# Router scores in a fused transformer block: two of the four groups of merged query weights kept as two rounded parts

## The reference

```python
h   = x * (1 + scale1) + shift1
z   = h @ w_in
# mixer A: gated 128x128 spatial MLP; mixer B: latent attention, 4 heads, up to 1152 keys
x   = LN1(alpha * x + gate1 * (concat(A, B) @ w_o))
h2  = x * (1 + scale2) + shift2
q   = (h2 @ w_pq).reshape(T, 8, 2, 128)
s   = einsum('thsd,hskd->thsk', q, sub_keys)      # 16 lists of 128 scores for each token
# top 16 of each list, top 16 of the 256 sums per head -> 128 of 16384 experts, softmax weights
x   = LN2(alpha * x + gate2 * sum_k w_k * gelu(u_k . h2) * v_k)
```

## Time and profile before

| | |
|---|---|
| runs before | 3253.39, 3255.07, 3258.79 us, median 3255.07 |
| the profiled execution | 3245.81 us, span 3244.0 us |
| PE busy over the span | 3159.9 us (97%) |
| DVE, ACT, POOL busy | 2594.7 (80%), 1253.2 (39%), 1617.1 us (50%) |
| mean granted TensorE clock | 0.992 |
| transfers | 979.82 MB, mean 302 GB/s |

### The profile page before, as it was taken

The page is one execution under the profiler, slowest core; times in us unless marked ns, Lnnn a source line. Parts: engine busy times, 40 slices in busy tenths (PEclk is TensorE's granted clock), DMA queues, the critical chain, the costliest instruction groups (busy, mean ns, idle before and its releaser), DMA issues.

```text
span 3244.0 us, 43176 instructions
## 1 busy us (share of the span) xinstructions
PE 3159.9 (97%) x15522; PEld 2625.2 (81%) x15522; DVE 2594.7 (80%) x5188; ACT 1253.2 (39%) x2305; POOL 1617.1 (50%) x1031
## 2 busy tenths in 40 slices
PE   8999899999988899999999999999999999999998
PEld 5887566665545699999999989989999999999997
DVE  3333138888889799999999889889999998888876
ACT  3343344333436633333343333333343333333343
POOL 0300113788777588888888887223333332233310
PEclk9999999999999999999999999999999999999999
DMA  6934866777677899999999999989899999999963
GB/s 248 390 117 159 326 221 195 208 220 193 198 214 227 283 349 348 349 351 356 351 339 349 357 358 387 370 337 370 340 371 362 352 366 356 354 364 357 345 227 118
DMA packets 300866, 979.82 MB, mean 302 GB/s; under 512 B 94580, under 2 KB 148724, under 8 KB 241399
## 3 DMA queue, kind: packets, MB, share of 16 engines
q1 hardware_dynamic: 159256, 532.10, 44.9%
q0 software_dynamic: 141120, 444.94, 39.4%
q10 hardware_dynamic: 288, 0.16, 0.0%
HBM read 902.22 MB, written 74.87 MB: 301 GB/s over the span
## 4 chain that ended last, share of the span: by engine, by line
PE 41%; POOL 18%; issue 3%; DVE 2%; DMA 1%; ACT 0%; DVEq 0%; ACTq 0%
PE scores L1952 21%; PE bank L1962 17%; POOL g_cells L189 12%; POOL ring L1914 6%; PE scores L1962 4%; DMA work<-in_u 1%; DVE ring L2100 0%; DVE uL L2283 0%; DVE acc L2117 0%; DMA ring<-in_uv,slots 0%; DVE vL L2279 0%; DVE slots L2222 0%; DVE ga L2296 0%; DVE st L2249 0%; DVE cL L2274 0%
## 5 line engine op out<-in xcount | busy, mean ns | idle before, releaser
L1914 POOL DMA_INDIRECT ring<-in_uv,slots x384 | 569.1, 1482 | 793.0 <-DVE carry L2117 695.1
L189 POOL DMA_INDIRECT g_cells<-slots x384 | 726.7, 1893 | 225.7 <-issue 115.9
L1952 PE MATMUL scores<-hR,uR 128*128 128x384 f32 x2032 | 682.2, 336 | 6.2 <-DVE uL L2283 6.2
L1952 PE MATMUL scores<-hR,uL 128*128 128x384 f32 x2032 | 682.0, 336 | 0.0
L1952 PE MATMUL scores<-hL,uR 128*128 128x384 f32 x2032 | 680.6, 335 | 0.0
L2039 ACT ACTIVATE cR<-ga 128x384 fp32r<-128x384 f32 x253 | 133.1, 526 | 942.8 <-PE bank L1962 547.6
L2100 DVE CUSTOM_DVE_ANT_0 ring<-ring,slots 128x1024 f32<-128x1024 f32 x384 | 467.5, 1254 | 17.6 <-DMA ring<-in_uv,slots 17.6
L1962 PE MATMUL bank<-vR,cR 128*128 128x512 f32 x1265 | 414.6, 392 | 0.0
L1962 PE MATMUL bank<-vR,cL 128*128 128x512 f32 x1265 | 412.7, 391 | 0.0
L1962 PE MATMUL bank<-vL,cR 128*128 128x512 f32 x1265 | 411.2, 390 | 0.0
L1952 PEld LDWEIGHTS scores<-hR,uR 128*128 128x128 f32 x2032 | 381.5, 188 | 18.4 <-DVE uL L2283 8.8
(11 more groups left out here) (370 smaller groups left out, 4593.9 us busy)
## 6 DMA issues: line engine op xcount, KB each, us to landing
work<-in_v SPq DMA_DIRECT2D x256, 512.0 KB
work<-in_u SPq DMA_DIRECT2D x254, 512.0 KB
work<-pq_scratch SPq DMA_DIRECT2D x36, 2048.0 KB
work<-in_w_o SPq DMA_DIRECT2D x18, 2048.0 KB
g_cells<-work POOLq DMA_DIRECT2D x48, 512.0 KB, 5.5
work<-g_cells SPq DMA_DIRECT2D x32, 768.0 KB
work<-g_blocks SPq DMA_DIRECT2D x31, 768.0 KB
g_blocks<-big SPq DMA_DIRECT2D x8, 2048.0 KB
```

The costliest lines, as they stand in the source:

```text
L189: pool.indirect_dma_start(out=cells_of(g_dram, i), out_offset=bass.IndirectOffsetOnAxis(ap=slots[:, i, D + k:D + k + 1].bitcast(U32), axis=0),
L1914: pool.indirect_dma_start(out=ring[:, k % R, :], out_offset=None, in_=a["uv"], in_offset=bass.IndirectOffsetOnAxis(ap=ids[:, k // P, k % P ...
L1952: mm = pe.matmul(A[t][:, 0:CW], w[t][:, k, :], h[:, k, :], start=(k == 0 and w is uR and h is hR), stop=(k == DK - 1 and w is uL))
```

## The change

Groups 2 and 3 of the merged weights (`SPLIT`) are no longer kept as float32 but as two fp32r parts. ACT copies each merged block rounded, DVE subtracts the rounded block from the same PSUM bank and only then frees the bank; POOL writes both parts to memory, a group being two halves of 2 MB, each with both parts of four blocks. A tile's transposed `h2` is split in the same way at h=0 of its tile i-2 (`parts`: ACT rounds, DVE subtracts). `score(i, 2)` and `score(i, 3)` then use 24 fp32r products in place of 8 float32 ones, the first 12 with one half, the others with the second. Each half is a number of its own in `WEIGHTS`, with the wait taken by the whole score that it follows. The staging of the merge has 8 buffers for groups 0 and 1, and 6 pairs for groups 2 and 3. The five reads of `mix_scratch` for tiles 2 to 6, which SP issued in slot 0 ahead of the keys, x and the first merge weights, are issued in slot 4, after the loads of `mix(0)`. A few waits for the merge's writes are added at first uses of the shared space (left out below).

```diff
+SPLIT = (2, 3)
...
+        pq_dram = [nc.dram_tensor("pq_scratch", [4, P, DK * 512], F32, kind="Internal").ap(),
+                   nc.dram_tensor("pq_parts", [len(SPLIT), 2, P, DK * 512], F32, kind="Internal").ap()]
...
+            w_parts = nc.alloc_sbuf_tensor_at("w_parts", [P, 2 * DK * 512], F32R, offset=work_at)
...
+            if key[0] == "score" and key[2] in SPLIT:
+                WEIGHTS.append((*key, 1))
...
+        merged = [front[:, at:at + 512] for at in (
+            *range(4 * D, 6 * D, 512), *range(9 * D, 10 * D, 512), *range(11 * D, 12 * D, 512))]
+        merged += [carry[:, at:at + 512] for at in range(0, 2 * D, 512)]
+        xR, xL = (x[:, :] for x in x_parts)
+        wp = w_parts[:, :].rearrange("p (b r c) -> p b r c", b=2, r=2)
...
+        MERGED = [0, 32, 64, 128, 192]
...
-                        sp.wait_ge(w_mm, W[WEIGHTS[at - 2]] + 1)
+                        sp.wait_ge(w_mm, W[WEIGHTS[at - 2][0:3]] + 1)
                     if key[0] == "score" and key[1] == 0:
                         for m_out in merged_out:
-                            sp.wait_ge(m_out, FILLED + 2 * (key[2] + 1) * 16)
+                            sp.wait_ge(m_out, FILLED + MERGED[key[2] + 1])
+                    if key[0] == "score" and key[2] in SPLIT:
+                        sp.dma_start(w_parts[:, at % 2 * DK * 512:(at % 2 + 1) * DK * 512].bitcast(F32),
+                                     pq_dram[1][SPLIT.index(key[2]), len(key) - 3, :, :]).then_inc(wr_in[at % 2], 16)
+                        return
                     part = key[1] if key[0] == "merge" else key[-1]
-                    src = {"mod": a["w_mod2"], "mix": a["w_o"], "merge": a["w_pqT"], "score": pq_dram}[key[0]]
+                    src = {"mod": a["w_mod2"], "mix": a["w_o"], "merge": a["w_pqT"], "score": pq_dram[0]}[key[0]]
...
-                        for t in range(2, LAST):
-                            sp.dma_start(slots[:, t, :], mix_dram[t, :, :]).then_inc(tile_in[2], 16)
...
+                    if n == H:
+                        for t in range(2, LAST):
+                            sp.dma_start(slots[:, t, :], mix_dram[t, :, :]).then_inc(tile_in[2], 16)
...
                     if h == 1 and 0 <= i - 2 < NT:
                         load("score", i - 2, 2)
+                        load("score", i - 2, 2, 1)
                     if h == 2 and 0 <= i - 2 < NT:
                         load("score", i - 2, 3)
+                        load("score", i - 2, 3, 1)
...
+                for g in range(4):
+                    for k in range(DK):
+                        pool.wait_ge(*emptied("merge", g, k))
+                        if g in SPLIT:
+                            for r_ in range(2):
+                                at = r_ * 4 * 512 + k % 4 * 512
+                                pool.dma_start(pq_dram[1][SPLIT.index(g), k // 4, :, at:at + 512],
+                                               merged[2 * (k % 6) + r_]).then_inc(merged_out[k // 2], 16)
+                        else:
+                            pool.dma_start(pq_dram[0][g, :, k * 512:(k + 1) * 512], merged[k]).then_inc(merged_out[k // 2], 16)
...
+                    if g in SPLIT:
+                        ps = bank("score", i, g)
+                        pe.wait_ge(x_low, i + 1)
+                        for half in range(2):
+                            at = WEIGHTS.index(("score", i, g, 1) if half else ("score", i, g)) % 2
+                            weights("score", i, g, *range(1, half + 1))
+                            for k in range(4):
+                                kk, sl = 4 * half + k, slice(k * 512, (k + 1) * 512)
+                                left = slice(kk * P, (kk + 1) * P)
+                                pe.matmul(ps[:, :], xR[:, left], wp[:, at, 0, sl], start=(kk == 0), stop=False)
+                                pe.matmul(ps[:, :], xR[:, left], wp[:, at, 1, sl], start=False, stop=False)
+                                mm = pe.matmul(ps[:, :], xL[:, left], wp[:, at, 0, sl], start=False, stop=(kk == DK - 1))
+                        mm.then_inc(w_mm, 1)
+                        return
...
                     for k in range(DK):
                         ps, f = bank("merge", g, k)
-                        x = DK * g + k
-                        if x >= 4:
-                            act.wait_ge(merged_out[x % 4], FILLED + x // 4 * 16)
-                        act.activation(merged[:, x % 4, :], ps[:, :], ACT.Copy).then_inc(f, 1)
+                        if g and k == 0:
+                            for m_out in merged_out:
+                                act.wait_ge(m_out, FILLED + MERGED[g])
+                        if g in SPLIT:
+                            if k >= 6:
+                                act.wait_ge(merged_out[0], FILLED + MERGED[g + 1])
+                            act.activation(merged[2 * (k % 6)].bitcast(F32R), ps[:, :], ACT.Copy).then_inc(merged_high, 1)
+                        else:
+                            act.activation(merged[k], ps[:, :], ACT.Copy).then_inc(f, 1)
+
+                def parts(i):
+                    if i == 0:
+                        act.wait_ge(w_mm, W["merge", 3, DK - 1] + 1)
+                    else:
+                        act.wait_ge(w_mm, W["score", i - 1, 3] + 1)
+                    act.activation(xR, slots[:, i, 0:D], ACT.Copy).then_inc(x_high, 1)
...
+                    if h == 0 and 0 <= i - 2 < NT:
+                        parts(i - 2)
...
+                def merge(g):
+                    for k in range(DK):
+                        w = W["merge", g, k]
+                        dve.wait_ge(merged_high, SPLIT.index(g) * DK + k + 1)
+                        dve.tensor_tensor(merged[2 * (k % 6) + 1].bitcast(F32R), PS[6 + w % 2][:, :], merged[2 * (k % 6)],
+                                          ALU.subtract).then_inc(free[w % 2], 1)
+
+                def parts(i):
+                    dve.wait_ge(x_high, i + 1)
+                    dve.tensor_tensor(xL, slots[:, i, 0:D], xR.bitcast(F32), ALU.subtract).then_inc(x_low, 1)
...
+                    if h == 0 and 0 <= i - 2 < NT:
+                        parts(i - 2)
                     if h == 0 and i >= 3:
                         decode(i - 3)
...
+                    if n in MERGE and MERGE[n] in SPLIT:
+                        merge(MERGE[n])
```

More of the change, by code:

```diff
@@ L161, in build @@
                 ("hR1", D, big_at, KT * H * P + 4 * 512), ("hL1", D, big_at, KT * H * P + 6 * 512))]
+            x_parts = [nc.alloc_sbuf_tensor_at(name, [P, D], F32R, offset=front_at + 4 * word) for name, word in (("xR", 0), ("xL", D))]
+            w_parts = nc.alloc_sbuf_tensor_at("w_parts", [P, 2 * DK * 512], F32R, offset=work_at)
             ga = nc.alloc_sbuf_tensor_at("ga", [P, 2, CW], F32, offset=big_at + 4 * KT * H * P * 2)
@@ L168, in build @@
             lists_of = middle(nc, a, sb, sem, PS, ident, modc, sp1, silu, slots, carry, work, first_in, big, krT, kT, vv, front, mod_in, x1_dram, gate_dram, g_dram, placed,
-                              mix_dram, tile_in, tile_out, a_mm, a_ev, g_in, ga, pq_dram, pool_out, scores_ps)
+                              mix_dram, tile_in, tile_out, a_mm, a_ev, g_in, ga, pq_dram, pool_out, scores_ps, x_parts, w_parts)
         experts(nc, a, sb, sem, PS, slots, carry, work, first_in, lists_of, x1_dram, g_dram, gate_dram, placed, a_mm, a_ev, g_in, ga, big_at)
@@ L716, in mixer_inputs, with middle @@
     return pool_out
-def middle(nc, a, sb, sem, PS, ident, modc, sp1, silu, slots, carry, work, first_in, big, krT, kT, vv, front, mod_in, x1_dram, gate_dram, g_dram, placed, mix_dram, tile_in, tile_out, a_mm, a_ev, g_in, ga, pq_dram, merged_out, scores_ps):
+def middle(nc, a, sb, sem, PS, ident, modc, sp1, silu, slots, carry, work, first_in, big, krT, kT, vv, front, mod_in, x1_dram, gate_dram, g_dram, placed, mix_dram, tile_in, tile_out, a_mm, a_ev, g_in, ga, pq_dram, merged_out, scores_ps, x_parts, w_parts):
     NH = NT * H
@@ L859, in middle @@
         w_mm, const_in, x1_out, gate_out = (sem(f"b_{n}") for n in ("wmm", "const", "x1out", "gateout"))
+        x_high, x_low, merged_high = (sem(f"b_{n}") for n in ("xhigh", "xlow", "mghigh"))
         row_in, x_in = ([sem(f"b_{n}{k}") for k in range(2)] for n in ("rowin", "xin"))
@@ L1310, in score @@
                         act.wait_ge(listed, 4 * (i - 1) + g + 1)
+                    elif g == 0:
+                        for m_out in merged_out:
+                            act.wait_ge(m_out, FILLED + MERGED[4])
                     act.activation(s[:, 4 * g:4 * g + 4, :], ps[:, :].rearrange("p (l k) -> p l k", l=4),
@@ L1320, in spread @@
                         for m_out in merged_out:
-                            act.wait_ge(m_out, FILLED + DK * 16)
+                            act.wait_ge(m_out, FILLED + MERGED[4])
                     sl = slice(4 * g, 4 * g + 4)
@@ L1580, in decode @@
                 def decode(i):
+                    if i == 0:
```

(2 more changed lines are left out.)

2 lines of the change are left out of this document (removed).

## The result

The changed kernel takes 3315.48 us (median of 4, 3310.52 to 3318.66) against 3254.70 us (median of 4): ratio 1.0185, 95% interval 1.017 to 1.0199, so 60.8 us slower. The forecast was 3291.6 us with a range up to 3312. The profiled execution took 3317.99 us with a span of 3315.8 us, 71.8 us above the span shown before.

A forecast was written before the change was run, and what follows sets the result against it. PE was taken to bound the experts, DVE and PE in turn tiles 3 to 8. Terms 18 + 1.5 + 26 - 9 = +36.5 us on 3255.07 gave 3291.6 us, range 3259 to 3312 (forecast's own 3280 to 3303).

The forecast's parts named there:

- `score(i, 3)` ... No wait: Steady tile: both halves of this score's weights arrive before they are wanted, at 694.7 and 699.7, so PE does not wait.
- the line behind it: Steady tile: next score(0) has its weights at 710.9 or 712.7 and starts at 711.0 or 712.7, against 709.28 before.
- The step above: Steady tile: score(i, 2) has its second half at 683.1, wanted at 683.9, and ends at 686.6.
- The split of x: Tiles 3 to 8: ACT's rounding and DVE's subtraction start decode and all behind it 1.75 us later.
- The idle at slot h=2 and the low clock behind it: Tiles 3 to 8: PE waits 3.7 us for DVE, then loses 1.8 us a tile to the clock (0 to 2.5).
- the term of 18 us: Tiles 3 to 8: six tiles at 3.0 us each make 18 us slower (10.5 to 24).
- Cheaper products buy nothing in the tiles: Tiles 3 to 8: a split score takes 5.5 us, 1.4 us less, but PE then waits for DVE.
- The tail: After the last attention slot: loads lie bare and the clock drops, 26 us slower (14 to 34) to the first scatter.
- The merges: merge(0) gains 7 us, merge(1) 4.5, merge(2) and merge(3) lose 2.5 for both; together -9 us (-12 to -4).
- Rival 4: Loads bind in each tile, a pair taking 16 us instead of 13: tiles 30, tail 32, 3310 us; chance 0.15.
- Rival 2: Faster: DVE has slack in tiles 3 to 8, so cheaper scores count; -11 us, 3244 us; chance 0.10.
- The low ends of the prediction's terms: Whole kernel: the lower bounds of the tiles, tile 2, tail and merge terms, said to add to +8.5 us.

The follow-up runs named there:

- e2: The changed kernel, with each half's load buffer given back when that half is read, not both at the score's end; 3284.73 us.
- e4: The changed kernel, with x split for tile 0 only and those parts used for all tiles; 3313.43 us.
- e5: The kernel before, with only the split of x added, scores still float32 and only waiting for the parts; 3270.54 us.
- e3: The changed kernel with both the edits of e1 and e2, early split of x and early release of the first half; 3273.61 us.
- e11: e3 with 1.2 us less DVE work in each tile, the multiplication by the first layer norm's gain left out; 3267.41 us.
- e6: The changed kernel without any split, leaving only the eight merge buffers and the mix_scratch reads in slot 4; 3245.21 us.
- e1: The changed kernel, with x split one slot earlier, at h=3 of the tile before instead of h=0; 3313.12 us.
- e10: The kernel before with 1.2 us less DVE work in each tile, the first layer norm's gain multiplication left out; 3254.13 us.

## Why the prediction was wrong

1. **The step that failed is "`score(i, 3)` ... No wait" and the line behind it,** by which the loads cost nothing in the tiles beyond what DVE cost. They cost 18.8 us in tiles 3 to 8 (after less e2; e4 without any split of x gives the same 18.8). The forecast had the second half there 0.4 us before it was wanted and the next weights 0.1 us before; that leaves no room for any delay. The step above was already off: it let `score(i, 2)` end 11.6 us after slot h=1, at 686.6, and it ended 13.3 us after, because its bank is freed by `residual_in`, which stands behind the split of x on DVE and was late by it. The prediction had moved `decode`, lists and `highest` by 1.75 us and forgotten who else reads what DVE releases. From there the chain is bare: both halves of `score(i, 3)` are issued when `score(i, 2)` ends at 705.9, the second is used at 719.73, 13.8 us on (forecast 13.1), and the next weights, issued at 722.79, are used 8.26 us on (forecast 8.1). The loads were sized nearly right; their sum became the tile's own path. Without the late bank (e4) the second half still comes 1.96 us late in tile 5 and the next weights 1.67 us: the loads bind by themselves, and the bank was not what made them. In tile 2 the same waits cost 5.3 us, 1.5 forecast, and with the earlier release (e2) none of it is left.
2. **The split of x: right, with one place missed.** +1.75 us a tile forecast, 10.6 us for six measured alone (e5), and 7.7 in e2, where the cheaper products are in too. The tail's 6.3 us in e5 were not in the forecast: there DVE is busy with lists when PE wants the parts.
3. **The idle at slot h=2 and the low clock behind it: did not come.** PE idles 1.80 us there and not 3.7, for the late bank had taken the rest ahead of it, and the clock stayed up in four of the six tiles. In tile 6 it fell twice, at other places (0.79 in 772 to 780 and in 804 to 812, behind waits of 2.40 and 2.20 us), and that tile took 77.10 us; in tile 8 once (0.57 in 940 to 944, behind 2.09 us), where the kernel before has one such stretch too. So the term of 18 us was 10.5 of split (10.6 alone, 7.7 in the changed kernel) and 7.5 of clock, mostly wrong, and 18.8 of loads were missing. That the term came within 9 us of the 26.5 is in part luck: a cost that did not come stood in for one that was left out.
4. **Cheaper products buy nothing in the tiles: right,** and e3 with e11 shows why: with all new waits for DMA gone a tile is still 67.7 us, and goes below that only when DVE has less to do. A split score took 5.6 us (700.25 to 705.9), forecast 5.5.
5. **The tail: right in size,** 27.3 against 26, with waits of 17.0 us for `pq_parts`, 6.9 for `pq_scratch` and 4.0 for DVE, and a granted clock of 0.81 from 1000 to 1072. Half of it goes with the earlier release (e2, 14.5). The waits above 4 us were two and not four, and the wait for DVE was not in the forecast, so the size is partly luck.
6. **The merges: the term was mis-sized,** -9 forecast, +0.9 measured. By slots: `merge(0)` gave 4.8 us (7 forecast), since it waits 1.65 us for a bank that ACT empties. `merge(1)` gave 0.5 (4.5 forecast): the moved reads made its load 2.1 us later, not 1, and the clock fell at the wait. For the split in `merge(2)` and `merge(3)` 2.5 us were forecast; they took 0.4 and 5.8 us more than before, and without the split (e6) 2.9 less and the same, so it cost 3.3 + 5.8 = 9.1 us. ACT and DVE empty a bank in turn, and in `merge(3)` ACT also waits 2.38 us for a write out of a buffer.
7. **Rivals.** Rival 4, at 3310 us, came nearest and has the right place, the loads in each tile, but not its reason: a pair took 12.9 to 13.8 us in the six tiles and not 16. Rival 2's one mechanism, slack on DVE, is refuted by e5 (the 1.75 us put on DVE in a tile show as 1.6 to 1.7) and e11. The low ends of the prediction's terms add to +12.5 us, not to +8.5.

What stays open: why e3's tail is 4.5 us longer than e2's, and how e1's gain divides. In the profiles e1 saves 7.2 us in tiles 3 to 8 against the changed kernel and e3 saves 7.5 against e2; the medians say 2.4 and 11.1, which their spread allows (in e1's profile the experts, which are not edited, took 6.2 us more than in the changed kernel's). And no run loads the halves into more than two buffers, so it is not shown whether the tail's waits could be hidden.

## What to carry to other kernels

When an operand grows to two loads, count from what event each buffer is given back: releasing each half when it is read was worth 31 us of the 61, at the cost of one increment. When work is put into an engine's program order, walk through everything behind it, also what only frees a bank. A saving on one engine counts only as far as the next engine's slack reaches: here it was below 0.3 us a tile (PE's 1.6 us of waits for `on` in six tiles before), so 2.8 us of products bought nothing. And a bulk read that is moved along a queue moved its delay to a load behind it in all three places tried; of the whole change only the extra buffers (with the reads in slot 4) are worth keeping, 3245.2 us.

## What the runs showed of the hardware

The clock of PE did not follow the length of an idle stretch. In the tail of the changed kernel the products behind 3.60 us of idle, at 990.22, ran at full pace for two steps; from the third on the step took 1.24 us and not 0.69. Behind only 2.09 us of idle, at 939.97, the second step was already slow. And behind the 1.7 to 1.8 us of idle for `on`, which five of the six tiles have, the clock stayed up each time. Timeline of PE, the first product of each step of three, at two places (0.39 us is full pace, 0.63 us the low level of 1.2 GHz):

```profile
939.97 0.50 PE L1137 MATMUL bank<-w_parts,xR 128*128 128x512 f32 x1 [2.09 <-DMA w_parts<-pq_parts]
...
940.96 0.63 PE L1137 MATMUL bank<-w_parts,xR 128*128 128x512 f32 x1
...
991.01 0.40 PE L1137 MATMUL bank<-w_parts,xR 128*128 128x512 f32 x1
...
991.70 0.59 PE L1137 MATMUL bank<-w_parts,xR 128*128 128x512 f32 x1
...
992.94 0.63 PE L1137 MATMUL bank<-w_parts,xR 128*128 128x512 f32 x1
```

The Trainium skill (TensorE: Matmul & The Clock Gate, "Part 1: The HAM clock gate (the 'warmup' mystery)") says that the gate judges activity on a free-running schedule of its own, so that the same code can lose a different number of products from run to run; the trace agrees so far as idles of one length had different effects: behind the 3.59 us ahead of 384.79 the products were slow at once, behind the 3.60 us ahead of 990.22 only from the third step on. A price for "the clock after such a wait" is then a chance and not a term.

A 2 MB load that PE waited for took 8.2 to 8.3 us from issue to use, in the tail (1012.34 to 1020.57) as in tile 5 (722.79 to 731.05), and 8.05 to 8.96 us over the six tiles. The estimate of 6.8 us from the Trainium skill (DMA: Bandwidth & Descriptors, "Anatomy of one DMA") is 1.4 us short of the first two; the page fits its figures to transfers that GpSimd issues, and these are issued by SP.

The experts' stretch took 2139 to 2143 us in three profiled executions (before, twice, and e10) and 2145 to 2152 in all others, with nothing changed in it. The medians of e5 and e6 leave no room for it, so it isn't counted here; no run explains it.
